# A pipeline over single experts in place of groups of three, with the sums in PSUM, ten ring units, and down weights asked for by ScalarE

## The reference

```python
for layer in range(DEPTH):
    i = layer // 2
    if layer % 2 == 0:
        h = h + even_mixer(rms_norm(h, mix_norm_even[i]), w_in_even[i], w_out_even[i])
    else:
        h = h + odd_mixer(rms_norm(h, mix_norm_odd[i]), w_in_odd[i], w_out_odd[i])
    h = h + hier_moe(rms_norm(h, ffn_norm[layer]), ...)
return rms_norm(h, final_norm)
```

```python
hid = jax.nn.silu(xb @ w_gate[e]) * (xb @ w_up[e])     # 1024 -> 512
return hid @ w_down[e]                                 # 512 -> 1024
```

## Time and profile before

| what | us |
|---|---|
| median of 3 runs | 1231.27 |
| lowest and highest run | 1230.86 and 1235.49 |
| the profiled execution, span | 1232.3 |
| TensorE busy | 1022.5 (83%) |
| VectorE busy | 421.3 (34%) |
| ScalarE busy | 208.8 (17%) |
| GpSimd busy | 36.6 (3%) |

### The profile page before, as it was taken

The page is one execution under the profiler, slowest core; times in us unless marked ns, Lnnn a source line. Parts: engine busy times, 40 slices in busy tenths (PEclk is TensorE's granted clock), DMA queues, the critical chain, the costliest instruction groups (busy, mean ns, idle before and its releaser), DMA issues.

```text
span 1232.3 us, 18607 instructions
## 1 busy us (share of the span) xinstructions
PE 1022.5 (83%) x7588; PEld 562.9 (46%) x7588; DVE 421.3 (34%) x1031; ACT 208.8 (17%) x531; POOL 36.6 (3%) x52
## 2 busy tenths in 40 slices
PE   8998988797787787787799999896977887877786
PEld 6874534442442442443378656344434433433442
DVE  5774522321321221222278735323212212221313
ACT  5643110100000000000155630001000000000101
POOL 1002000000000000000010210000000000000000
PEclk9999999998998898898889998999988998997988
DMA  9856389999999999999945543999999999999992
GB/s 358 285 212 266 137 343 419 418 430 418 418 427 423 419 423 424 419 421 421 362 165 239 225 168 124 376 419 416 428 422 420 423 425 419 421 426 420 419 421 106
DMA packets 76307, 441.25 MB, mean 358 GB/s; under 512 B 8816, under 2 KB 8816, under 8 KB 59760
## 3 DMA queue, kind: packets, MB, share of 16 engines
q1 hardware_dynamic: 76128, 440.26, 87.6%
q10 hardware_dynamic: 144, 0.52, 0.1%
HBM read 439.72 MB, written 1.05 MB: 358 GB/s over the span
## 4 chain that ended last, share of the span: by engine, by line
PE 51%; DMA 39%; DVE 6%; ACT 2%; issue 1%; SPq 1%; POOL 1%; DVEq 0%; ACTq 0%; POOLq 0%
DMA ring<-in_w_expert_down 38%; PE bank L736 12%; PE bank L887 11%; PE bank L867 5%; PE bank L924 4%; PE bank L759 3%; PE bank L761 3%; PE bank L760 3%; PE bank L835 2%; PE bank L917 2%; PE bank L898 1%; PE bank L957 1%; DMA ring<-in_w_in_even 1%; PE bank L810 1%; DVE work L1098 1%
## 5 line engine op out<-in xcount | busy, mean ns | idle before, releaser
L867 PE MATMUL bank<-ring,work 128*32 128x256 f32 x4096 | 249.6, 403 | 43.6 <-DMA ring<-in_w_expert_up 43.2
L867 PEld LDWEIGHTS bank<-ring,work 128*32 128x32 f32 x4096 | 141.8, 116 | 138.9 <-issue 67.6
L736 PE MATMUL bank<-cst 128*128 128x512 f32 x252 | 156.6, 785 | 42.1 <-DMA ring<-in_w_expert_down 42.1
L887 PE MATMUL bank<-ring,work 128*32 128x512 f32 x960 | 141.3, 594 | 0.0
L1296 DVE COPY work<-bank 96x512 f32<-96x512 f32 (+1 forms) x22 | 15.1, 687 | 350.6 <-PE bank L887 337.5
L736 PEld LDWEIGHTS bank<-cst 128*128 128x128 f32 x252 | 62.0, 256 | 119.3 <-issue 119.3
L835 PE MATMUL bank<-work,xn 128*128 128x96 f32 (+1 forms) x704 | 88.6, 287 | 22.9 <-DVE work L1264 22.9
L835 PEld LDWEIGHTS bank<-work,xn 128*128 128x128 f32 x704 | 84.9, 201 | 41.2 <-DVE work L1264 41.2
L917 PE MATMUL bank<-work 96*128 96x512 f32 (+1 forms) x176 | 85.1, 615 | 15.7 <-ACT work L620 15.7
L1290 DVE TENSOR_SCALAR work<-work 128x128 f32<-128x128 f32 x64 | 14.5, 226 | 224.5 <-ACT work L615 224.5
L887 PEld LDWEIGHTS bank<-ring,work 128*32 128x32 f32 x960 | 37.5, 110 | 100.8 <-issue 100.8
(11 more groups left out here) (145 smaller groups left out, 781.9 us busy)
## 6 DMA issues: line engine op xcount, KB each, us to landing
ring<-in_w_expert_gate SPq DMA_DIRECT2D x64, 2048.0 KB, 26.4
ring<-in_w_expert_up SPq DMA_DIRECT2D x64, 2048.0 KB, 30.1
ring<-in_w_expert_down SPq DMA_DIRECT2D x62, 2048.0 KB, 27.6
ring<-in_w_in_even SPq DMA_DIRECT2D x5, 2048.0 KB, 18.0
ring<-in_w_in_odd SPq DMA_DIRECT2D x5, 2048.0 KB, 20.9
ring<-in_w_out_even SPq DMA_DIRECT2D x2, 2048.0 KB, 8.3
ring<-in_w_expert_down SPq DMA_DIRECT2D x4, 1024.0 KB, 18.2
ring<-in_w_out_odd SPq DMA_DIRECT2D x2, 2048.0 KB, 8.4
```

What stands on the lines that cost most here:

```text
L736: pe.matmul(psum[7][:, :], data[:, 0:P], data, start=True, stop=True)
L867: last = pe.matmul(bank[32 * j:32 * j + 32, 0:2 * P].rearrange("p (a s) -> p a s", a=2), xT[:, c, SLOTS * k:SLOTS * k + SLOTS], ring[:, 2 ...
L887: last = pe.matmul(psum[6 + half][32 * k:32 * k + 32, :], hidT[k][:, 32 * j:32 * j + 32], ring[:, 6 + k, D * j + 512 * half:D * j + 512 * ...
```

## The change

The mixture becomes a pipeline over single experts, in eight groups of four (GE = 4) that only share the gather.

- The ring has ten units. The pairs of gate and up lie at units 0, 2, 4 and 7 (and the unit behind each), the downs at units 9 and 6 in turn. w_out lies in units 9 and 6.
- TensorE's order for expert e is gate_up(e + 2), down(e), scatter(e). Behind the second expert of a group it gathers for the next group. keep_warm leaves the expert loop.
- SyncE asks for the pair of expert e + 4 when gate_up(e) is done. ScalarE asks for down e + 2 on its own queue when down(e) is done, ahead of its copy of y.
- A row of down is read as `(p j) n -> p (j n)`, one piece of 16 KB for a partition. The hidden units are then spread over the partitions in another order, which one VectorE transpose in 32 by 32 blocks gives; TensorE's transpose of hid and ScalarE's copy of it leave.
- The down products of an expert use four column tiles, one for each quarter of the hidden width, each into rows of its own; `gated` is repeated four times along the slots, so that the scatter sums the quarters. It is made for one expert at a time.
- h is put into four PSUM banks at the start of the mixture by products with the identity (`start_sums`), and every scatter adds there. VectorE's adds into h leave. Behind the last expert of layer 0, ScalarE and VectorE copy the four banks to h; behind layer 1 the squares and the final scaling read PSUM.
- The last group of a layer, in which nothing is loaded ahead, stands behind the branch around the later rounds.

```diff
-GE = 3
-FULL = EXPERTS // GE
-TAIL = EXPERTS - FULL * GE
+GE = 4
+GROUPS_OF = EXPERTS // GE
+AHEAD = 2
+UNITS = 10
+PAIR_AT = (0, 2, 4, 7)
+DOWN_AT = (9, 6)
+W_OUT_AT = DOWN_AT
...
-            down_rows = w_down.rearrange("l e (j p) n -> (l e) p j n", p=P)
+            down_rows = w_down.rearrange("l e (p j) n -> (l e) p (j n)", p=P)
...
+            def load_pair(l, row, k):
+                unit = PAIR_AT[k]
+                sp.dma_start(ring[:, unit, :], gate_rows[row]).then_inc(pair_arrived[l][k], 16)
+                sp.dma_start(ring[:, unit + 1, :], up_rows[row]).then_inc(pair_arrived[l][k], 16)
...
+            def load_group(l, r, g):
+
+                for k in range(GE):
+                    sp.wait_ge(gate_up_done[l], expert_no(r, g, k) + 1)
+                    load_pair(l, l * EXPERTS + GE * g + (GE + k), k)
...
+            def finish_expert(l, e, b, next_row):
+
+                act.wait_ge(gated_turned[l], e + 1)
+                act.copy(gatedT, psum[7][:, 0:SEQ]).then_inc(gatedT_ready[l], 1)
+                act.wait_ge(down_done[l], e + 1)
+                if next_row is not None:
+                    act.dma_start(ring[:, DOWN_AT[b], :], down_rows[next_row]).then_inc(down_arrived[l][b], 16)
+                act.copy(y_sb[:, 0:512], psum[4][:, :]).then_inc(y_low[l], 1)
...
+            def down(l, r, g, k):
+
+                e = expert_no(r, g, k)
+                pe.wait_ge(gated_ready[l], e + 1)
                 for t in range(T):
+                    last = pe.transpose(psum[7][:, P * t:P * t + P],
+                                        gated[k][:, t, :, :].rearrange("p b s -> p (b s)"), ident)
                 last.then_inc(gated_turned[l], 1)
+                pe.wait_ge(hidT_ready[l], e + 1)
+                pe.wait_ge(down_arrived[l][k % 2], (r * (EXPERTS // 2) + g * (GE // 2) + (k // 2 + 1)) * 16)
+                for half in range(2):
+                    for j in range(4):
+                        last = pe.matmul(
+                            psum[4 + half][32 * j:32 * j + 32, :], hidT[k][:, 32 * j:32 * j + 32],
+                            ring[:, DOWN_AT[k % 2], D * j + 512 * half:D * j + 512 * half + 512],
+                            start=True, stop=True, tile_position=(0, 32 * j))
+                last.then_inc(down_done[l], 1)
+
+            def scatter(l, e, last):
+
+                pe.wait_ge(gatedT_ready[l], e + 1)
+                pe.wait_ge(y_low[l], e + 1)
+                pe.wait_ge(y_high[l], e + 1)
+                for t in range(T):
+                    for half in range(2):
+                        pe.matmul(acc[t][half][:, :], gatedT[:, P * t:P * t + P], y_sb[:, 512 * half:512 * half + 512],
+                                  start=False, stop=last).then_inc(scattered[l], 1)
...
+            def group(l, r, g, after):
+
+                for k in range(GE):
+                    if k < GE - AHEAD:
+                        gate_up(l, r, g, k + AHEAD)
+                    elif after:
+                        gate_up(l, *after, k - (GE - AHEAD))
+                    down(l, r, g, k)
+                    scatter(l, expert_no(r, g, k), not after and k == GE - 1)
+                    if k == GE - AHEAD - 1 and after:
+                        gather(l, group_no(*after))
...
+            def hidden(l, e, k):
+
+                chain = Chain(dve, dve_moe[l], e * SILU_LINKS)
+                dve.wait_ge(gate_up_out[l], e + 1)
+                eb, gb, hb = eg[k % 2], gu[k % 2], hid[k % 2]
+                chain.link(dve.tensor_scalar(eb, eb, 1.0, None, ALU.add))
+                chain.link(dve.reciprocal(eb, eb))
+                chain.link(dve.tensor_tensor(eb, eb, gb[:, 0:P], ALU.mult))
+                assert chain.n == SILU_LINKS
+                dve.tensor_tensor(hb, eb, gb[:, P:2 * P], ALU.mult).then_inc(hid_ready[l], 1)
+                dve.wait_ge(hid_ready[l], e + 1)
+                dve.transpose(hidT[k].rearrange("p (b s) -> p b s", b=4),
+                              hb.rearrange("p (a b) -> p b a", b=4)).then_inc(hidT_ready[l], 1)
```

433 lines of the change are left out of this document (186 added, 247 removed).

## The result

The changed kernel takes 1218.6 us, the median of four runs from 1211.6 to 1220.0, beside 1231.1 us before: ratio 0.988, 95% interval 0.984 to 0.992. Forecast were 1209 us in a range from 1201 to 1230, so the sign is right, the time inside the range and 9.6 us above the forecast. The profiled execution took 1217.5 us, its span 1215.2 instead of 1232.3.

A forecast was written before the change was run, and what follows sets the result against it. The DMA transfers of expert weights were taken as the bound. Twice minus 18.7 us plus 15.2 for the tails is minus 22.2 from the 1232.3 span, 1210.1; less 1.0 for the median, 1209 us, range 1201 to 1230.

The forecast's parts named there:

- Rate: In the expert loops, weights arrive at 430 GB/s instead of 422 with 16 KB down pieces; 7.9 us per layer.
- The rule of 512 B: Skill's least transfer size for full DMA rate; by it longer down pieces gain nothing, 422 GB/s stays, 1225 us.
- T31: Landing of each layer's last gate and up pair, forecast 415.2 us behind the first refill of the ring.
- each byte behind the restart: Weights still to load at a layer's first ring refill; 4.6 MB less were to save 10.8 us per layer.
- TensorE's turn: One expert's cycle on TensorE in the loop: 12.2 us against 14.6 of DMA, so 2.4 us of slack.
- ScalarE's DMA: ScalarE's issue of each down ahead of its y copy: 0.4 us taken, bounds 0.39 and 5.65.
- rival (d): ScalarE's down issue blocks; at 5.2 us each it costs 78 us, 1287 us; chance 0.06.
- The tail: Each layer's end behind the last pair's landing: 32.5 us in layer 0, 36.0 in layer 1, plus 15.2 in all.
- The branch: TensorE's pause at skipped later rounds, now before the last group: 2.8 us per layer, bounds 0 and 5.2.
- (a): Rival: piece length does not matter in weight transfers, 422 GB/s stays, 1225 us; chance 0.07.
- (b): Rival: ScalarE's queue is served behind SyncE's, layer 0's last scatter about 19 us later, 1228 us; chance 0.05.
- (c): Rival: pauses without keep_warm lower TensorE's clock in the expert loop, making it the bound, 1243 us; chance 0.09.

The follow-up runs named there:

- the long row alone: The kernel before, with only down's rows read as one 16 KB piece per partition, hidden units meeting wrong rows: 1220.2 us, ratio 0.990.
- one loop: The changed kernel with TensorE's branch around the later rounds replaced by a single loop over all rounds' groups: 1212.2 us, ratio 0.982 to the kernel before.
- the late pair: The changed kernel with expert 3's gate and up asked for only behind gate_up(0), eight ring units there at the first refill, not ten: 1235.9 us, ratio 1.002.
- the run with four: The changed kernel with each down asked for as four 512 KB transfers instead of one: 1298.4 us, ratio 1.052 to the kernel before.

## Why the prediction was right, and where its sizes were off

*Rate.* Right, and the main term: 7 us per layer for the long row alone. The size: 428 GB/s, not 430. For 177.9 MB that is 1.9 us per layer. The rule of 512 B that the prediction weighed (the Trainium skill, DMA: Bandwidth & Descriptors, Specifications) is not borne out, and the prediction was right to go by its rows: with both queues at 4 KB the rate is 410 GB/s, with 16 KB 428.

*T31, the landing of the last pair.* Forecast 415.2 us behind the refill; with one loop, in layer 1, gate_up(31) waits for it until 1176.24, 417.6 behind 758.67. Of the 2.4 us, 1.9 are the rate, and so the sharing of the two queues in equal parts was right. It was an assumption without a row when it was made; the shares of the pieces bear it out for pieces of one length, and for no others. That each byte behind the restart counts is what the late pair showed.

*TensorE's turn.* 12.2 us forecast; scatter(1) to scatter(5) of layer 0 take 48.67 us, 12.17 each, while the ring is still full. From start to start gate_up took 3.6 (3.5), from its end to scatter 4.15 (4.3), scatter 3.6 (3.4), gather 0.9 per expert (1.0). The wait before scatter was 1.8 and not 2.2, since down took 1.92 instead of 1.7 and VectorE was a little earlier, though its 32 by 32 transpose took 0.40 us instead of 0.3. The prediction's own terms from the end of gate_up to the y copy add up to 4.0 and not to its 4.3; the 0.3 in between has no row, and 4.15 was measured. Two of its signs came out smaller than forecast. The wait for up is 76.4 us, 1.4 for each of 56 experts and not 2 to 3. gate_up is 3.66 us without a wait before it, 5.0 to 6.6 behind 16 of 18 waits of 2.1 to 7.0 us, and 4.2 on average: the lower clock took a part of the slack.

*ScalarE's DMA.* 0.34 us per issue in the median and 0.40 at most (0.4 taken). What a long issue costs was seen in the run with four. The bound of 5.65 us for rival (d) was too low for what its own trace shows: it is the longest issue of a gate, and single downs of 512 pieces held SyncE for up to 16.2 us.

*The tail.* From gate_up(31) to the last scatter 24.7 us where 24.0 was worked out, the same in both layers. From there to the projection 5.3 us (5.7; the terms listed for it add up to 5.6 without the copy of h and 6.2 with it), to the end of the span 9.0 (9.2). The upper end of the forecast's own range, 1221, is 2 us more than its terms give (1209 + 4.8 + 5).

*The branch.* This is the term that was wrong in each layer: "5.2 us less the slack of 2.4 there: 2.8". It was 5 in layer 0 and nothing in layer 1, so that only their sum (5.6 forecast, 5.0 measured) came out, by luck. In layer 0 the slack did cover most of the first pause, but there was a second, which the prediction did not have. With one loop gate_up(30) waits for its pair and starts 403.9 us behind the refill, with the branch 405.2: 1.3 us of the first pause of 4.02 count. The second, 3.15 us, counts in full, and the products of gate_up(30) take 7.24 us in place of 6.58. Together these are the 5.0. In layer 1 TensorE had 6.01 us to wait for pair 30 in any case.

In layer 1 gate_up(31) started 2.0 us late and the tail took 0.7 more, and the 2.8 that were not needed made up for both, so that the forecast of 442.0 against 441.9 is partly luck. In layer 0 gate_up(31) would start 3.0 us late without the branch (about 2.0 of rate, the rest gate_up(30) at the lower clock), the branch adds 5.0, the tail 0.7, less the 2.8 taken: the 5.9 us over the forecast. Without the branch the span is 1209.9, by chance the 1210.1 of the sum.

*The 9.6 us.* The spans are 5.1 us over the forecast: layer 0's 5.9, less 0.8 in the other stretches. The other 4.5 us of the 9.6 have no cause in the kernel: the two profiled executions lie on different sides of their medians.

*Where the gain is from.* Spans: 1232.3 before, 1217.9 with the long row alone, 1209.9 with the new pipeline and one loop, 1215.2 as changed. So 14.4 us are the row (12.7 by the medians); the pipeline brings 8.0, of which 5.6 lie between the last scatter of layer 0 and the projection (10.9 to 5.3 us), where the branch stood before and cost 6.05 us in the run with the long row; 5.3 are given back through the branch's new place. As changed, the pipeline and its second queue bring 2.7 us by the spans and 1.6 by the medians, which is no more than what the groups differ by. The sum had little for it as well: fewer bytes behind the restart, minus 21.6, and the longer tail behind the last pair, plus 15.2 with the branch, leave 6.4.

*Rivals.* (a) fell with the long row alone. (b) fell with the landings: 13.7 us beside 44.5. (c) The clock rose from 0.92 to 0.95 though keep_warm is gone, and TensorE did not become the bound. Its mechanism is there, though: the gate_ups that follow a long wait run mostly at the lower level (with one loop 6.58 us behind 4.41 of waiting, at a granted clock of 0.54, and 3.66 without a wait), and they cost 28.7 us of TensorE's time, all but about 1 us of it covered by slack. (d) did not occur with one transfer of long rows.

## What to carry to other kernels

When weights set the time, look at the length of each piece per partition before the order of the work: here the longer piece gave more than the rewritten pipeline. Two queues share by pieces and not by bytes, so a queue whose data is awaited soonest must have pieces as long as its neighbour's; and when both queues and an engine reach the end together, shortening one of them alone is worth nothing. A skipped branch belongs where its engine waits for something else for longer than its instructions take to come, or gives way to a loop whose count is worked out.

## What was not expected of the hardware

- One queue with 4 KB pieces beside one with 16 KB: 53% of the pieces, 22% of the bytes, landing 26.0 us instead of 13.7; with 4 KB on both 48% of either and 14.5.
- 16 KB pieces ran at 428 GB/s, 4 KB pieces at 410, on both queues; 4 KB downs among 16 KB pairs in one queue at 422 over the long stretch.
- A matmul whose moving operand is read at a stride of 16 bytes: mean 634 ns for 256 columns with four column tiles side by side, contiguous 383 to 422; busy time of the group 474.4 us instead of 249.6.
- Four issues of 128 pieces each held ScalarE 1.83 us, and its next copy started 3.34 us after its last work; one issue held it 0.34. A down of 512 pieces held SyncE for up to 16.2 us while its queue was long, with the DMA engines busy throughout.
- Pauses of 4.02 and 3.15 us of TensorE around a branch that skips the later rounds, the second in the middle of 64 products; 16 KB of instructions landed 1.8 and 1.3 us before it went on.
